# Gated delta rule inverse: levels 1 to 4 on 32 by 32 blocks in four places of the array, level 5 between blocks only

## Chip, cores, metric

One core of one Trainium2 chip runs the whole kernel in one launch. The metric is the device time in microseconds (us), of which the profile's span (first to last instruction) is nearly all.

## The reference, cut to what matters

The kernel computes six layers on 256 tokens of width 1024: a chain of four mixers (gated deltanet, HGRN2, GLA, gated deltanet), each followed by a SwiGLU block, and then two layers of another block. The change touches only the two gated deltanet ("gdn") layers, and in them only the inverse of a unit lower triangular matrix:

```
L = jnp.where(strict, jnp.einsum('bhncd,bhnsd->bhncs', kb, k) * decay, 0.0)
rhs = jnp.concatenate([v * beta[..., None], kb * jnp.exp(G)[..., None]], axis=-1)
sol = lax.linalg.triangular_solve(L + jnp.eye(CHUNK, dtype=F32), rhs, left_side=True, lower=True)
```

The kernel takes chunks of 128 tokens where the reference takes 64. So a gdn layer has 16 such matrices of 128 by 128: 8 heads times 2 chunks, numbered j, in four groups g of four.

## The kernel before

The inverse X of I + L is built by doubling. When X holds the inverses of the diagonal blocks of size 2^lv, level lv adds what couples two neighbours, by X - X C X, where C is L masked to that coupling (`level64`). Level 0 is I - C without a product. Levels 1 to 5 work on the two diagonal 64 by 64 blocks of each matrix. The two blocks lie on partitions 0 to 63 and 64 to 127 (`blocks`, line 336), so each product is issued twice, once for each block. Level 6 couples the two 64 blocks.

A level of one group g passes through the engines so:

- PE, line 894: C X, "cx", 4 matrices x 2 blocks = 8 matmuls into one PSUM bank.
- ACT, line 1427: copies the bank to `cx` (in `yb`).
- PE, `gdn_correct`, line 968: both X (CX) and its transpose, "z", 4 matrices x 2 forms x 2 blocks = 16 matmuls into one bank. X and its transpose XT are kept side by side in `inv` (`xx`).
- DVE, line 1903: subtracts the bank from X and XT, 128x512 at once. At level 5 it is three operations, and XT lands in the full-size matrices `inv[:, 16 + j, :]`, whose rest POOL has cleared (line 1415).
- POOL, line 1420: masks L for the next level into `lb_masked`, 4 matrices at a time, once cx of that group is done.

PE issues cx of group g and then z of group g - 1, so that ACT and DVE work on one group while PE works on another. At a level's start it issues cx of groups 0 and 1 and then waits for ACT's copy of group 0. Ahead of level 1, ACT copies the diagonal blocks of L to `lb`, POOL masks them, DVE forms XT of level 0, PE transposes it (line 949) and ACT copies it to X. Level 6 (lines 897 and 963) multiplies 64 by 64 blocks; behind it stand lines 907, 914 and 922, which apply the inverse to the values, on full 128 by 128 matrices.

A matmul in f32 is done in two passes; the trace has one record for the weight load and one for the product of each pass, so that x4 in a timeline row is two matmuls. Order is fixed by the program on each engine, and by semaphores between them. The function `stay_awake` issues products that nothing reads; there are none between levels 1 and 6.

Of the kernel before, what the change touches and what calls it, by code (L numbers as in the profile page):

```python
# [26 lines left out]
ALU = mybir.AluOpType  # L27
# [17 lines left out]
HALF2 = HALF // 2  # L45
TRI = 3 * HALF
# [166 lines left out]
def build(nc, A, out, book, layers=len(CHAIN)):  # L213

    book.restart()
    with ExitStack() as ctx:
# [47 lines left out]
        level64 = sb("level64", [P, 6, HALF2])  # L264
        ident64 = sb("ident64", [P, HALF2])

# [67 lines left out]

        cx = flat(yb)[:, 0:16 * HALF2].rearrange("p (j n) -> p j n", j=16)
        blocks = (slice(0, HALF2), slice(HALF2, HALF))
        xx = flat(inv[:, 0:16, :]).rearrange("p (g two j n) -> p g two j n", g=4, two=2, j=4)
        lb_masked, lb = (flat(ct)[:, 16 * HALF2 * n:16 * HALF2 * (n + 1)].rearrange("p (j n) -> p j n", j=16) for n in range(2))

        def inverse(j):  # L340


            return xx[:, j // 4, 0, j % 4, :]
# [151 lines left out]
        def _(pe):  # L495
# [353 lines left out]
            def gdn(layer):  # L849
# [34 lines left out]
                for lv in range(1, 7):  # L884
                    for g in range(4):
                        b = psum.claim(pe, "cx", layer, lv, g)
                        if lv < 6:
                            pe.wait_ge(*pool_gdn.at("masked", layer, lv, g))
                        pe.wait_ge(*(act_gdn.at("X", layer, g) if lv == 1 else dve_gdn.at("X", layer, lv - 1, g)))
                        for j in range(4 * g, 4 * g + 4):  # L890
                            cols_of = slice((j % 4) * HALF2, (j % 4 + 1) * HALF2)
                            if lv < 6:
                                for r in blocks:
                                    m = nc.tensor.matmul(b[r, cols_of], lb_masked[r, j, :], inverse(j)[r, :], start=True, stop=True)  # L894
                            else:
                                t0 = (j // 8) * T
                                m = nc.tensor.matmul(b[HALF2:HALF, cols_of], lt[0:HALF2, j % 8, t0 + HALF2:t0 + HALF], inverse(j)[0:HALF2, :],
                                                     start=True, stop=True)
# [44 lines left out]
            def gdn_transpose(layer, g):  # L943
# [3 lines left out]
                for j in range(4 * g, 4 * g + 4):  # L947
                    for r in blocks:
                        m = nc.tensor.matmul(b[r, (j % 4) * HALF2:(j % 4 + 1) * HALF2], transposed(j)[r, :], ident[r, r],
                                             start=True, stop=True)  # L950
                m.then_inc(*pe_gdn.tick("transposed", layer, g))

            def gdn_correct(layer, lv, g):
# [4 lines left out]
                if lv == 6:  # L958
                    pe.wait_ge(*dve_gdn.at("XT", layer, 5, g))
                for j in range(4 * g, 4 * g + 4):  # L960
                    c = (j % 4) * HALF2
                    if lv == 6:
                        m = nc.tensor.matmul(b[0:HALF2, c:c + HALF2], cx[HALF2:HALF, j, :], inv[HALF2:HALF, 16 + j, HALF2:HALF],
                                             start=True, stop=True)
                        continue
                    for left, right, c in ((transposed(j), cx[:, j, :], c), (cx[:, j, :], transposed(j), c + T)):
                        for r in blocks:
                            m = nc.tensor.matmul(b[r, c:c + HALF2], left[r, :], right[r, :], start=True, stop=True)  # L968
# [354 lines left out]
        def _(pool):  # L1323
# [83 lines left out]
            for layer, (kind, _) in enumerate(CHAIN[:layers]):  # L1407
# [7 lines left out]
                g.memset(inv[:, 16:32, 0:HALF2], 0.0).then_inc(*pool_gdn.tick("cleared", layer))  # L1415
                for lv in range(6):
                    for q in (0, 2, 1, 3) if lv == 0 else range(4):
# [3 lines left out]
                                        level64[:, lv:lv + 1, :].to_broadcast([P, 4, HALF2]), ALU.mult)\  # L1421
                            .then_inc(*pool_gdn.tick("masked", layer, lv, q))

        @block.scalar
        def _(act):
# [277 lines left out]
            def gdn(layer, l):  # L1703
# [16 lines left out]
                for g in (0, 2, 1, 3):  # L1720
                    act.wait_ge(*pe_gdn.at("transposed", layer, g))
                    run(s, group(g, 0), psum.bank("transposed", layer, g)[:, 0:T], ACT.Copy, "X", layer, g)
                    psum.release(s, "transposed", layer, g)
                for lv in range(1, 7):
                    for g in range(4):
                        act.wait_ge(*pe_gdn.at("cx", layer, lv, g))
                        rows_of = slice(0 if lv < 6 else HALF2, HALF)
# [886 lines left out]
```

## Time and profile before

| | us |
|---|---|
| median of 3 runs | 2289.57 |
| lowest and highest | 2284.36, 2289.63 |
| the profiled execution: its time | 2284.88 |
| its span | 2282.9 |
| mean granted TensorE clock over the span | 0.976 |

PE is matmuls, PEld weight loads, DVE the vector engine, ACT the scalar engine, POOL GpSimd. A stretch of the span is given as from:to in us from its start. The first gdn layer's inverse lies at 150 to 189, the second's at 1242 to 1281. "x" behind a busy time counts records.

### The profile page before, as it was taken

To read this page: it belongs to the slowest core of one execution; us is meant where nothing else is said; L and a number is where in the kernel's file an instruction comes from. 1 tells how busy PE (TensorE), PEld (TensorE's weight loads), DVE (VectorE), ACT (ScalarE), POOL (GpSimd) and SP (SyncE) were. 2 spreads that over 40 slices of the span, in tenths; PEclk is the share of its full clock that TensorE was granted. 3 is DMA by queue.
4 is the path that set the end of the run, shared out by engine and by line. 5 is a ranking of instruction groups with operands and counts; after the bars stand their busy time and mean duration, and the time that the engine had idled before them with its cause. 6 is when DMAs were issued, how large, how long until landed. Compare 5 with 4: busy or idle time off the path is not lost.

```text
span 2282.9 us, 35627 instructions
## 1 busy us (share of the span) xinstructions
PE 2172.9 (95%) x14401; PEld 1878.3 (82%) x14401; DVE 1497.0 (66%) x1925; ACT 883.7 (39%) x1153; POOL 210.2 (9%) x176
## 2 busy tenths in 40 slices
PE   7999999999999999999899999989789998979999
PEld 7988788898788788888798878869379997748998
DVE  6857654778744748554785664454677886367887
ACT  2243444232344322444314344444553334554332
POOL 5720000000000000000272100000210000030000
PEclk9999999999999999999999999999889999979999
DMA  7511655551555543665451165536025554403552
GB/s 213 182 41 57 203 185 186 175 184 46 201 185 185 167 155 99 198 193 168 148 185 57 39 209 186 184 117 196 1 84 180 190 174 138 137 10 129 185 184 93
DMA packets 265605, 333.81 MB, mean 146 GB/s; under 512 B 16492, under 2 KB 228593, under 8 KB 265473
## 3 DMA queue, kind: packets, MB, share of 16 engines
q1 hardware_dynamic: 265473, 331.93, 45.1%
q8 instruction: 98, 1.61, 0.3%
q14 instruction: 34, 0.28, 0.1%
HBM read 330.84 MB, written 1.05 MB: 145 GB/s over the span
## 4 chain that ended last, share of the span: by engine, by line
PE 86%; DVE 6%; ACT 4%; issue 2%; POOL 1%; SPq 0%; DMA 0%; POOLq 0%; DVEq 0%; ACTq 0%
PE bank L550 44%; PE bank L522 28%; PE bank L968 2%; PE bank L594 2%; PE bank L1023 1%; PE bank L584 1%; PE bank L741 1%; PE bank L894 1%; ACT w_hi L1473 1%; ACT stat L1427 1%; ACT mats L1427 1%; ACT xh L1427 1%; PE bank L847 1%; PE bank L833 1%; DVE xt L1913 1%
## 5 line engine op out<-in xcount | busy, mean ns | idle before, releaser
L1949 DVE TENSOR_TENSOR w_lo<-ring,w_hi 128x2048 fp32r<-128x2048 f32 (+2 forms) x297 | 627.6, 2115 | 356.9 <-ACT w_hi L1473 354.3
L1473 ACT ACTIVATE w_hi<-ring 128x2048 fp32r<-128x2048 f32 (+1 forms) x222 | 417.8, 1882 | 485.4 <-PE bank L550 302.2
L550 PE MATMUL bank<-w_lo,xh 128*128 128x512 f32 x992 | 268.7, 393 | 0.0
L550 PE MATMUL bank<-w_hi,xh 128*128 128x512 f32 x928 | 251.1, 392 | 10.6 <-ACT xh L1427 6.8
L550 PE MATMUL bank<-w_hi,xl 128*128 128x512 f32 x928 | 249.0, 390 | 0.0
L522 PE MATMUL bank<-xh,w_hi 128*128 128x256 f32 (+1 forms) x1816 | 243.6, 288 | 4.7 <-DVE w_hi L1947 4.7
L522 PE MATMUL bank<-xh,w_lo 128*128 128x256 f32 (+2 forms) x1880 | 245.3, 283 | 0.0
L522 PEld LDWEIGHTS bank<-xh,w_hi 128*128 128x128 f32 (+1 forms) x1816 | 230.7, 193 | 11.7 <-issue 4.5
L522 PE MATMUL bank<-xl,w_hi 128*128 128x256 f32 (+1 forms) x1816 | 237.2, 283 | 0.0
L522 PEld LDWEIGHTS bank<-xh,w_lo 128*128 128x128 f32 (+2 forms) x1880 | 232.1, 188 | 2.2 <-issue 0.2
L522 PEld LDWEIGHTS bank<-xl,w_hi 128*128 128x128 f32 (+1 forms) x1816 | 225.7, 190 | 0.7
L550 PEld LDWEIGHTS bank<-w_lo,xh 128*128 128x128 f32 x992 | 186.1, 189 | 38.1
L550 PEld LDWEIGHTS bank<-w_hi,xh 128*128 128x128 f32 x928 | 173.4, 189 | 49.9 <-issue 11.6
L550 PEld LDWEIGHTS bank<-w_hi,xl 128*128 128x128 f32 x928 | 174.7, 188 | 36.7
L1386 POOL TENSOR_TENSOR w_lo<-ring,w_hi 128x1536 fp32r<-128x1536 f32 x28 | 112.5, 4017 | 998.6 <-DVE w_hi L1947 998.6
L550 PE MATMUL bank<-w_hi,hid_hi 128*128 128x512 f32 x528 | 169.2, 402 | 8.1 <-DVE hid_lo L1903 8.1
L550 PE MATMUL bank<-w_hi,hid_lo 128*128 128x512 f32 x528 | 164.9, 394 | 0.0
L550 PE MATMUL bank<-w_lo,hid_hi 128*128 128x512 f32 x528 | 164.3, 393 | 0.0
L1427 ACT ACTIVATE yb<-bank 128x256 f32<-128x256 f32 (+4 forms) x146 | 59.0, 404 | 180.2 <-PE bank L550 125.0
L550 PEld LDWEIGHTS bank<-w_hi,hid_lo 128*128 128x128 f32 x528 | 100.2, 190 | 21.9
L550 PEld LDWEIGHTS bank<-w_lo,hid_hi 128*128 128x128 f32 x528 | 100.0, 189 | 21.9
L550 PEld LDWEIGHTS bank<-w_hi,hid_hi 128*128 128x128 f32 x528 | 95.5, 191 | 26.7 <-DVE hid_lo L1903 10.7
(314 smaller groups left out, 2504.4 us busy)
## 6 DMA issues: line engine op xcount, KB each, us to landing
ring<-in_ffn_w_in_dram SPq DMA_DIRECT2D x264, 512.0 KB, 4.4
ring<-in_ffn_w_down_dram SPq DMA_DIRECT2D x88, 512.0 KB, 4.2
ring<-in_gdn_w_in_dram SPq DMA_DIRECT2D x64, 512.0 KB, 5.0
ring<-in_ffn_w_out_dram SPq DMA_DIRECT2D x44, 512.0 KB, 3.9
ring<-in_w_in_dram SPq DMA_DIRECT2D x36, 512.0 KB, 4.7
ring<-in_hgrn_w_in_dram SPq DMA_DIRECT2D x32, 512.0 KB, 4.6
ring<-in_gla_w_in_dram SPq DMA_DIRECT2D x24, 512.0 KB, 4.7
ring<-in_gdn_w_out_dram SPq DMA_DIRECT2D x16, 512.0 KB, 4.1
```

The source lines that it names most:

```text
L522: m = nc.tensor.matmul(cols, *((wk, xk) if tokens == ALL else (xk, wk)), start=(first and step == 0 and k == 0 and (j % 2 == 0)), stop=(la ...
L550: m = nc.tensor.matmul(bank[:, 0:width], xin[:, k0 + k, rows_of], w[:, k, c * width:(c + 1) * width], start=(first and step == 0 and k == ...
L584: m = nc.tensor.transpose(b[:, j * P:(j + 1) * P], src[:, t, c * CHUNK + j * P:c * CHUNK + (j + 1) * P], ident[:, :])
L594: m = nc.tensor.matmul(b[:, 0:T], ones[:, :], strict[:, 0:T], start=True, stop=True)
L741: m = nc.tensor.transpose(banks[6][:, j * T + t * HALF:j * T + (t + 1) * HALF], hidt[:, t, j * P:(j + 1) * P], ident[:, :])
L833: nc.tensor.matmul(b[:, 0:T], k[:, 0:HALF], q[:, :], start=True, stop=True)
L847: nc.tensor.matmul(b[:, :], ones[:, :], gsq(g), start=True, stop=True).then_inc(*pe_gdn.tick("qk2", layer, g))
L968: m = nc.tensor.matmul(b[r, c:c + HALF2], left[r, :], right[r, :], start=True, stop=True)
L1386: g.tensor_tensor(w_lo[:, unit % RING, part], ring[:, unit % RING, part], high_part(unit)[:, part], ALU.subtract).then_inc(*pool_lo.tick())
L1427: nc.scalar.activation(out_, in_, func, **kw).then_inc(*sig.tick(*key))
L1473: nc.scalar.activation(high_part(u)[:, 0:n], ring[:, u % RING, 0:n], ACT.Copy).then_inc(*act_hi.tick())
L1949: v.tensor_tensor(w_lo[:, u % RING, 0:share], w[:, 0:share], high[:, 0:share], ALU.subtract).then_inc(*dve_lo.tick())
```

## The change

Levels 1 to 4 now work on the four diagonal 32 by 32 blocks of a matrix (`blocks` has four entries, and `level32`, `ident32` and `lb` are half as wide). Each product is issued four times, at rows and columns 0, 32, 64 and 96 of the array. The banks, copies, masks and subtractions of these levels cover half as many columns.

Level 5 computes only what lies between two 32 blocks of a 64 block. cx: 8 matmuls of 32 by 32 for a group, straight from `lt`, without a mask. z: 12 matmuls, three for each matrix. ACT copies two 32x128 pieces of a group, DVE writes three pieces of 32x128, one of them into a new full 64 by 64 place for X, `x64`, and two into the full-size XT.

The diagonal 32 blocks are brought to those places by POOL: six copies behind level 4, on which cx of level 6 waits ("assembled"). POOL no longer masks for level 5, and clears 128x2048 and 32x16x32 values where it cleared 128x1024.

On PE, in level 1, group 0's z before:

```order
113 L968 MATMUL bank<-yb,inv 64x64 x2
114 L968 MATMUL bank<-inv,yb 64x64 x2
115 L968 MATMUL bank<-yb,inv 64x64 x2
116 L968 MATMUL bank<-inv,yb 64x64 x2
117 L968 MATMUL bank<-yb,inv 64x64 x2
```

and now, at the same place:

```order
112 L900 MATMUL bank<-inv,ct 32x32 x32
113 L980 MATMUL bank<-yb,inv 32x32 x4
114 L980 MATMUL bank<-inv,yb 32x32 x4
115 L980 MATMUL bank<-yb,inv 32x32 x4
116 L980 MATMUL bank<-inv,yb 32x32 x4
```

Nothing changed places; there are twice as many matmuls, each of a quarter of the elements. On PE at level 5 and the start of level 6, now (L903 is cx, L974 and L976 are z, L906 is cx of level 6):

```order
261 L903 MATMUL bank<-inv,mats 32x32 x8
262 L974 MATMUL bank<-yb,inv 32x32
263 L976 MATMUL bank<-inv,yb 32x32 x2
...
285 L974 MATMUL bank<-yb,inv 32x32
286 L976 MATMUL bank<-inv,yb 32x32 x2
287 L906 MATMUL bank<-inv,mats 64x64 x8
```

The last of level 5 is followed at once by cx of level 6, as before. On POOL, the first layer's inverse before:

```order
44 L1415 MEMSET inv 128x16x64
45 L1420 TENSOR_TENSOR ct<-ct,level 128x256 x24
```

and now:

```order
44 L1427 MEMSET inv 128x2048
45 L1428 MEMSET inv 32x16x32
46 L1433 TENSOR_TENSOR ct<-ct,level 128x128 x20
47 L1439 COPY inv<-inv 32x16x32 x2
48 L1441 COPY inv<-inv 32x16x32 x4
```

Four masks are gone, and six copies stand behind the rest. The diff, cut to its core:

```diff
-        level64 = sb("level64", [P, 6, HALF2])
+        level32 = sb("level32", [P, 5, BLOCK])
...
-        blocks = (slice(0, HALF2), slice(HALF2, HALF))
+        cx64 = flat(yb)[:, 8 * HALF:8 * HALF + 16 * HALF2].rearrange("p (j n) -> p j n", j=16)
+        blocks = [slice(BLOCK * n, BLOCK * (n + 1)) for n in range(4)]
+        pairs = (blocks[0], blocks[1]), (blocks[2], blocks[3])
+        xx = flat(inv[:, 0:8, :]).rearrange("p (g two j n) -> p g two j n", g=4, two=2, j=4)
+        x64 = flat(inv[:, 8:16, :]).rearrange("p (j n) -> p j n", j=16)
...
-                        if lv < 6:
+                        if lv < 5:
                             pe.wait_ge(*pool_gdn.at("masked", layer, lv, g))
+                        if lv == 6:
+                            pe.wait_ge(*pool_gdn.at("assembled", layer))
...
+                            elif lv == 5:
+                                for of, to in pairs:
+                                    m = nc.tensor.matmul(b[to, n * BLOCK:(n + 1) * BLOCK], lt[of, j % 8, t0 + to.start:t0 + to.stop],
+                                                         inverse(j)[of, :], start=True, stop=True)
...
-                if lv == 6:
-                    pe.wait_ge(*dve_gdn.at("XT", layer, 5, g))
...
+                    elif lv == 5:
+                        r = blocks[1]
+                        m = nc.tensor.matmul(b[r, c:c + BLOCK], transposed(j)[r, :], cx[r, j, :], start=True, stop=True)
+                        for to, r in pairs:
+                            m = nc.tensor.matmul(b[to, c + HALF:c + HALF + BLOCK], cx[r, j, :], transposed(j)[r, :], start=True, stop=True)
...
-                g.memset(inv[:, 16:32, 0:HALF2], 0.0).then_inc(*pool_gdn.tick("cleared", layer))
-                for lv in range(6):
+                g.memset(inv[:, 16:32, :], 0.0).then_inc(*pool_gdn.tick())
+                g.memset(x64[blocks[0], :, BLOCK:HALF2], 0.0).then_inc(*pool_gdn.tick("cleared", layer))
+                for lv in range(5):
...
+                pool.wait_ge(*dve_gdn.at("X", layer, 4, 3))
+                for r in blocks[:2]:
+                    g.tensor_copy(x64[r, :, r].rearrange("p (g j) n -> p g j n", g=4), xx[r, :, 0, :, :]).then_inc(*pool_gdn.tick())
+                for r in blocks:
+                    g.tensor_copy(inv[r, 16:32, r].rearrange("p (g j) n -> p g j n", g=4), xx[r, :, 1, :, :])\
+                        .then_inc(*pool_gdn.tick("assembled", layer))
...
+                            for r in (slice(0, HALF),) if lv < 5 else (pairs[0][1], pairs[1][1]):
+                                run(s, flat(cx[r, 4 * g:4 * g + 4, :]), b[r, 0:HALF], ACT.Copy, "cx", layer, lv, g)
...
-                            tt(s, group(g, 0), group(g, 0), b[:, 0:T], ALU.subtract, "X", layer, lv, g)
-                            for r in blocks:
-                                tt(s, inv[r, 16 + 4 * g:16 + 4 * g + 4, r], xx[r, g, 1, :, :],
-                                   b[r, T:2 * T].rearrange("p (h n) -> p h n", h=4), ALU.subtract, "XT", layer, lv, g)
+                            dve.wait_ge(*pool_gdn.at("cleared", layer))
+                            r = blocks[1]
+                            ts(s, x64[r, 4 * g:4 * g + 4, blocks[0]], b[r, 0:HALF].rearrange("p (h n) -> p h n", h=4), -1.0, ALU.mult)
+                            for to, r in pairs:
+                                ts(s, inv[to, 16 + 4 * g:16 + 4 * g + 4, r], b[to, HALF:T].rearrange("p (h n) -> p h n", h=4),
+                                   -1.0, ALU.mult, None, None, "X", layer, lv, g)
```

## Rows read from the trace of the kernel before

**Rows 1.** The page: busy us (share) xinstructions; the chain that ended last.
```profile
PE 2172.9 (95%) x14401; PEld 1878.3 (82%) x14401; DVE 1497.0 (66%) x1925; ACT 883.7 (39%) x1153; POOL 210.2 (9%) x176
...
PE 86%; DVE 6%; ACT 4%; issue 2%; POOL 1%; SPq 0%; DMA 0%; POOLq 0%; DVEq 0%; ACTq 0%
```

**Rows 2.** Stretches: length, busy PE, PEld, DVE, ACT, POOL, clock, DMA, GB/s.
```profile
150.00:154.64 4.64, 4.03 (x74) 3.36 (x74) 2.21 (x4) 2.81 (x7) 3.17 (x5) 1.00 0.00 0
154.64:178.88 24.24, 23.71 (x776) 23.09 (x772) 10.28 (x15) 6.54 (x17) 12.79 (x19) 1.00 0.02 4
178.88:185.31 6.43, 5.91 (x196) 5.66 (x193) 3.58 (x10) 1.54 (x4) 0.00 (x0) 1.00 0.01 3
185.31:189.10 3.79, 3.74 (x77) 3.48 (x74) 3.08 (x8) 1.52 (x4) 0.00 (x0) 1.00 0.02 4
1246.40:1271.24 24.84, 24.04 (x775) 23.29 (x772) 10.33 (x15) 6.53 (x17) 12.76 (x18) 1.00 0.02 4
1271.24:1276.96 5.72, 5.62 (x193) 5.51 (x190) 3.50 (x9) 1.54 (x4) 0.00 (x0) 1.00 0.02 6
1276.96:1280.80 3.84, 3.79 (x80) 3.53 (x75) 3.11 (x8) 1.52 (x4) 0.00 (x0) 1.00 0.00 0
```

**Rows 3.** Timeline of PE in level 2 (start, length, x passes).
```profile
162.28 0.33 PE L968 MATMUL bank<-yb,inv 64*64 64x64 f32 x4
...
163.23 0.66 PE L894 MATMUL bank<-inv,ct 64*64 64x64 f32 x16
```

**Rows 4.** Timeline of PE where level 5 meets level 6.
```profile
185.36 0.22 PE L968 MATMUL bank<-yb,inv 64*64 64x64 f32 x1
185.42 0.22 PE L897 MATMUL bank<-inv,mats 64*64 64x64 f32 x1
185.42 0.22 PE L968 MATMUL bank<-inv,yb 64*64 64x64 f32 x2
185.48 0.22 PE L897 MATMUL bank<-inv,mats 64*64 64x64 f32 x1
185.48 0.22 PE L968 MATMUL bank<-inv,yb 64*64 64x64 f32 x1
185.53 0.92 PE L897 MATMUL bank<-inv,mats 64*64 64x64 f32 x13
```

**Rows 5.** Timeline at the start of level 2, PE and ACT.
```profile
161.05 1.13 PE L894 MATMUL bank<-inv,ct 64*64 64x64 f32 x32
...
161.75 0.85 ACT L1427 ACTIVATE yb<-bank 128x256 f32<-128x256 f32 x2 [2.39 <-PE bank L894]
```

**Rows 6.** Groups by shape, ACT and DVE (xcount | busy us, mean ns | idle).
```profile
L1427 ACT ACTIVATE yb<-bank 128x256 f32<-128x256 f32 x128 | 49.2, 384 | 166.8 <-PE bank L550 125.0 <-PE bank L894 40.8
L1427 ACT ACTIVATE ct<-bank 128x512 f32<-128x512 f32 x8 | 4.8, 598 | 9.7 <-PE bank L922 5.3 <-PE bank L907 4.3
L1903 DVE TENSOR_TENSOR inv<-inv,bank 128x512 f32<-128x512 f32 x32 | 22.0, 688 | 30.2 <-PE bank L968 30.2
L1907 DVE TENSOR_SCALAR inv<-bank 64x256 f32<-64x256 f32 x8 | 3.3, 417 | 1.5 <-PE bank L963 1.2
```

**Rows 7.** Groups by shape: POOL.
```profile
L1420 POOL TENSOR_TENSOR ct<-ct,level 128x256 f32<-128x256 f32 x48 | 34.8, 740 | 52.7 <-ACT ct L1427 31.2 <-PE bank L894 21.2
L1396 POOL TENSOR_TENSOR sq<-sq,trig 128x512 f32<-128x512 f32 x4 | 5.6, 1395 | 686.5 <-PE bank L1104 686.5
L1415 POOL MEMSET inv<- 128x1024 f32 x2 | 1.9, 951 | 48.7 <-ACT dec L1427 48.7
```

**Rows 8.** Stretches with PE nearly idle, and what followed.
```profile
1104.60:1107.49 2.89, 0.00 (x0) 0.00 (x0) 2.85 (x5) 2.40 (x2) 0.00 (x0) 1.00 0.73 238
1107.49:1114.32 6.83, 4.34 (x19) 2.88 (x20) 5.48 (x9) 1.69 (x4) 0.00 (x0) 0.50 0.00 0
2046.40:2048.20 1.80, 0.16 (x4) 0.11 (x4) 1.76 (x4) 0.19 (x1) 1.57 (x1) 1.00 0.00 0
```

**Rows 9.** DMA queues, 154.6 to 185.3: packets, MB, share of 16 engines.
```profile
q8 instruction: 7, 0.11, 1.8%
```

More of the change, by code:

```diff
@@ L45 @@
 HALF2 = HALF // 2
+BLOCK = HALF2 // 2
 TRI = 3 * HALF
@@ L333, in u @@
             return ct[:, 8 * t + h, :]
-        cx = flat(yb)[:, 0:16 * HALF2].rearrange("p (j n) -> p j n", j=16)
-        blocks = (slice(0, HALF2), slice(HALF2, HALF))
-        xx = flat(inv[:, 0:16, :]).rearrange("p (g two j n) -> p g two j n", g=4, two=2, j=4)
-        lb_masked, lb = (flat(ct)[:, 16 * HALF2 * n:16 * HALF2 * (n + 1)].rearrange("p (j n) -> p j n", j=16) for n in range(2))
+        cx = flat(yb)[:, 0:16 * BLOCK].rearrange("p (j n) -> p j n", j=16)
+        cx64 = flat(yb)[:, 8 * HALF:8 * HALF + 16 * HALF2].rearrange("p (j n) -> p j n", j=16)
[3 more added lines that the diff above has]
+        x64 = flat(inv[:, 8:16, :]).rearrange("p (j n) -> p j n", j=16)
+        lb_masked, lb = (flat(ct)[:, 16 * BLOCK * n:16 * BLOCK * (n + 1)].rearrange("p (j n) -> p j n", j=16) for n in range(2))
         def inverse(j):
@@ L1721, in gdn @@
                     act.wait_ge(*pe_gdn.at("transposed", layer, g))
-                    run(s, group(g, 0), psum.bank("transposed", layer, g)[:, 0:T], ACT.Copy, "X", layer, g)
+                    run(s, group(g, 0), psum.bank("transposed", layer, g)[:, 0:HALF], ACT.Copy, "X", layer, g)
                     psum.release(s, "transposed", layer, g)
@@ L1726, in gdn @@
                         act.wait_ge(*pe_gdn.at("cx", layer, lv, g))
-                        rows_of = slice(0 if lv < 6 else HALF2, HALF)
-                        run(s, flat(cx[rows_of, 4 * g:4 * g + 4, :]), psum.bank("cx", layer, lv, g)[rows_of, 0:T], ACT.Copy,
-                            "cx", layer, lv, g)
+                        b = psum.bank("cx", layer, lv, g)
+                        if lv == 6:
+                            run(s, flat(cx64[HALF2:HALF, 4 * g:4 * g + 4, :]), b[HALF2:HALF, 0:T], ACT.Copy, "cx", layer, lv, g)
+                        else:
+                            for r in (slice(0, HALF),) if lv < 5 else (pairs[0][1], pairs[1][1]):
+                                run(s, flat(cx[r, 4 * g:4 * g + 4, :]), b[r, 0:HALF], ACT.Copy, "cx", layer, lv, g)
                         psum.release(s, "cx", layer, lv, g)
@@ L2276, in gdn @@
                             X = xx[:, g, :, :, :].rearrange("p two j n -> p (two j n)")
[L2277 removed]
+                            tt(s, X, X, b[:, 0:T], ALU.subtract, "X", layer, lv, g)
                         elif lv == 5:
[L2279 to L2282 removed]
+                            dve.wait_ge(*pool_gdn.at("cleared", layer))
[4 more added lines that the diff above has]
+                                   -1.0, ALU.mult, None, None, "X", layer, lv, g)
                         else:
```

37 lines of the change are left out of this document (18 added, 19 removed).

## The prediction, made before the changed kernel ran

> **What bounds the kernel now.** I read the page's busy times and its chain first, then the busy time of each engine by stretch, then the timeline inside one level. PE is busy for 95% of the span and makes up 86% of the chain that ended last [rows 1], so a change on PE counts where it stands. In levels 1 to 4 PE is busy 23.71 of 24.24 us in the first layer and 24.04 of 24.84 in the second, at the full clock, with DVE under half and POOL at about half [rows 2]. A level takes 24.54 / 4 = 6.1 us on average of both layers. Level 5 takes 6.43 and 5.72 us, level 6 3.79 and 3.84 [rows 2]. The stage is bound by the pace of PE's passes, and all that it saves should reach the end, since PE is the bound behind it too.
>
> The pace: 32 passes of z start from 162.28 to 163.23, 0.0297 us each, 0.059 us for a matmul of two passes [rows 3]. A level has 96 matmuls: 5.7 us, and 0.4 is left for the wait at its start. Where only one place of the array is in use, 13 passes of level 6 take 0.92 us, the last of them 0.22 us long: (0.92 - 0.22) / 12 = 0.058 us a pass [rows 4]. So two places at once halve the time of a pass: a place is busy 0.058 us with 64 columns, and two places don't disturb each other.
>
> **Levels 1 to 4.** They have twice the matmuls, 192 a level, each 32 columns wide in one of four places. How long such a pass holds its place isn't in the trace. If it goes with the columns, it is 0.029 us; four places at once then give 0.0073 us a pass and 0.015 us a matmul. That is the lower end. The upper end within this mechanism is the shortest mean distance at which passes are seen to start: where three places are in use, three start within 0.06 us (at 185.42 twice in L968 and once in L897, then again at 185.48) [rows 4], so 0.0195 us a pass and 0.039 us a matmul. But those three stand within 0.01 us of each other and the rest is the place being busy, so issue isn't what spaced them. I take 0.020 us a matmul, nearer the lower end for that reason: 192 x 0.020 = 3.84 us.
>
> To this comes the wait at a level's start. Before, cx of groups 0 and 1 is issued from 161.05, so group 0's last pass starts at about 161.5; ACT starts its copy at 161.75, two copies take 0.85 us [rows 5], and z starts at 162.28 [rows 3], 0.8 us after group 0's last pass and 0.3 us after group 1's. Now ACT copies 128 columns: from 384 ns at 256 columns and 598 at 512 [rows 6] I work out 0.28 us, so z can start 0.68 us after group 0's last pass, of which group 1's cx covers 16 x 0.020 = 0.32. The wait is 0.36 us. All other waits are covered: DVE's subtraction of 256 columns takes 0.42 us (417 ns for 256, 688 for 512 [rows 6]), and between a z and the cx that needs it PE has at least 2 us of other groups; POOL's mask of 128 columns takes at most the 0.74 us of 256 [rows 7], 3.0 us for four against 4.2. A level is then 3.84 + 0.36 = 4.2 us, four are 16.8, against 24.54: 7.7 us less for a layer.
>
> PE's code has to be fetched too. From 154.6 to 185.3 there are 7 instruction packets in 1.8% of 16 engines' 30.7 us [rows 9], 1.26 us each, for some 450 matmuls, so 64 to a packet. 768 matmuls need 12 packets, 15.1 us: under 16.8, if they follow each other directly. The Trainium skill says how large they are ("Runtime: NRT & Kernel Launch", section Instruction fetch mechanics): blocks of 256 instructions, fetched while the others run, hidden by an issue floor of about 20 cycles an instruction. By that floor four instructions for a matmul would take longer than the 0.059 us that the trace shows now, so the trace doesn't agree with the floor, and the cover that the page speaks of may go.
>
> **Ahead of level 1.** ACT's copies of the last diagonal blocks double in number at 0.28 instead of about 0.4 us each: 1.1 instead of 0.8 us for a group, so 0.7 later over the last two. Against it stand POOL's shorter masks (two, up to 0.25 each), DVE's subtraction (0.14 less), and 64 transposes at 0.020 instead of 32 at 0.059: 0.6 less. I take 0.3 us less; bounds 0.6 less and 0.7 more. The longer clearing costs nothing: POOL idles 48.7 us ahead of the two it has now, and they take 0.95 us each [rows 7].
>
> **Levels 5 and 6.** PE's part shrinks from 96 to 80 matmuls, in two places or one: a z group of 12 holds its busiest place for 4 x 2 x 0.029 = 0.23 us, as long as cx. All together PE has 1.9 us, with waits for ACT's eight copies (2.2 us) 3.3 us. DVE's twelve pieces at 0.28 us are 3.4 us and end 5 us after level 5 began, though only the last group's are needed late. But now level 6 waits for POOL. X of level 4's last group is ready 0.7 us after cx of level 5 starts (z ends, 0.25 to DVE, 0.42 for it), and then come six copies of 512 values in each of 32 partitions. The trace has no POOL copy. Its bounds are half of clearing 1024 values, 0.48 us, and the product of two inputs of 512 values, 1.40 us [rows 7]. I take 0.85, between them, since a copy reads one input where the product reads two. So level 6 starts at 0.75 + 6 x 0.85 = 5.85 us, rounded up to 6.0 for the waits on both sides; bounds 5.0, where DVE is last, and 9.2. Level 6 itself stays at 3.8 us: 9.8 against 10.22 and 9.56 before, mean 9.9. So what level 5 saves on PE turns into a wait for POOL: 0.1 less.
>
> **The clock.** PE has nothing to do from 3.3 to 6.0 us, 2.7 us. In the trace a granted clock of 1.00 fell to 0.50 behind 2.89 us without a pass, for 6.83 us, and stayed at 1.00 behind 1.80 us in which PE was busy 0.16 [rows 8]. 2.7 us with a thin stretch ahead lies nearer the first, so I take the fall to half, the level at 1.2 GHz. Up to 3.4 of the 6.83 us are lost then; level 6 and what follows are bound by PE for some 0.7 of the time, so 2.4 us more for a layer (bounds 0 and 3.4).
>
> **The sum.** A layer: -7.7 - 0.3 - 0.1 + 2.4 = -5.7 us; both -11.4. The profiled execution of 2284.9 us would be 2273.5, its span 2271.5. That execution lies 4.7 us under the median of 2289.57, so beside the median the forecast is 2278.2 us, 0.5% less.
>
> **Rivals.** The first: the clock doesn't fall. Then it is -8.1 a layer, 2273.4 us. For it: the gap is somewhat shorter than the 2.89 us.
>
> The second: POOL eats the gain. With 1.40 us a copy level 6 starts 3.2 us later in each layer, and the clock falls for certain with up to 1.0 us more: -11.4 + 8.4 gives 2286.6 us, no change that can be told. For it: nothing in the trace shows a strided copy of 32-wide pieces. Against it: the 1.40 us belong to two inputs. The same time results if a matmul costs 0.030 us in the levels (0.010 x 192 x 4 = 7.7 us a layer, less the shorter wait).
>
> The third ends slower: the starts of passes have a spacing of their own on PE, however many places are free. It decides from the point where four levels lose the 5.7 us: (22.5 / 4 - 0.36) / 192 = 0.0274 us a matmul, 0.0137 a pass. The trace shows no mean under 0.0195 [rows 4]. With that as the spacing, a level is 192 x 0.039 + 0.3 = 7.8 us, four are 31.2, 6.7 more than before; with +2 for the rest of the layer it is about 2307 us. The same mechanism at its worst is that the four places don't work at once at all, so that the change doesn't do what its words say: 4 x 0.0073 = 0.029 us a pass, as now with two, 0.058 a matmul, 11.5 us a level, 2289.6 + 2 x (21.5 + 2) = 2337 us. Against it speaks that passes for different places start within 0.01 us of each other [rows 4].
>
> The Trainium skill has such a rule ("TensorE: Matmul & The Clock Gate", section Wait — 56ns, not 53.3ns?): start to start never drops under about 25 ns, however narrow the product. The starts that lie closer in the rows speak against it holding between places. By that figure, as an estimate, a level would take some 10 us and the kernel about 2325 us. Its section on packing small matmuls says the opposite, a start each 4 ns between places.
>
> **How the numbers follow.** The forecast's mechanism, with the clock falling in at least one of the layers, has 0.42; the clock staying up, 0.18; POOL or the pace eating the gain, 0.20; the third rival 0.20. The measurement of this kernel tells 0.3% from no change, so faster is under 2282.7 us and slower over 2296.4. Faster has the first two, 0.60, same 0.21, slower 0.19. The range leaves out most of the third rival and reaches from 2264 (0.015 us a matmul, 13.2 us for four levels, though fetching holds it at 15.1; POOL at its lower bound; no fall of the clock: -1.7 beyond -8.1 for the pace and -1.0 for POOL in each layer, and some margin) to 2294 (POOL's upper bound and a pace of 0.025 together).
>
> **What would show it.** In the changed profile: four levels in 16.8 us and z passes for four places starting within 0.04 us; ACT's copies of 128 columns at 0.28 us; six POOL copies of 0.85 us behind level 4 with cx of level 6 right behind the last; DVE done before it; the granted clock at 0.5 in about 187 to 194. The prediction is wrong if levels take over 22 us, if a POOL copy takes over 1.2 us, or if level 6 waits for another engine.

## The result, and the profile after

The changed kernel takes 2335.2 us (median of 4 runs, 2332.5 to 2337.0) beside 2288.9 us for the kernel before in the same comparison: a ratio of 1.0206, with a 95% interval of 1.0188 to 1.0223. It is slower by 2.1%, far outside the spread of either kernel. The forecast was 2278.2 us with a range of 2264 to 2294, so the sign is wrong and the time lies outside the range.

The page after shows the busy time and share of each engine, the queue of instruction packets, and the chain that ended last. Its first and last line answer to [rows 1]; the packets' line of the page before stands below.

```profile
PE 2177.7 (93%) x16001; PEld 1877.8 (81%) x16001; DVE 1484.8 (64%) x1929; ACT 883.5 (38%) x1177; POOL 200.3 (9%) x182
...
q8 instruction: 111, 1.82, 0.3%
...
PE 84%; DVE 7%; ACT 4%; issue 4%; POOL 1%; SPq 0%; DMA 0%; DVEq 0%; POOLq 0%; ACTq 0%
```

```profile
q8 instruction: 98, 1.61, 0.3%
```

PE is busy hardly longer than before (2177.7 us against 2172.9), although the run is 46 us longer. What grew in the chain is "issue", time in which PE waited for nothing that the profile shows: from 2% to 4%. Instruction packets went from 98 to 111 for 800 more matmuls (half of the 1600 more records), which fits 64 matmuls a packet. The loss is small on the page because the page averages over the whole span. Stretch by stretch it can't be missed. These rows answer to [rows 2], with the same columns: ahead of level 1, levels 1 to 4 in two pieces, level 5, level 6, what follows, and then levels 1 to 4, 5 and 6 of the second layer.

```profile
150.00:154.30 4.30, 3.18 (x138) 2.54 (x139) 1.52 (x4) 3.07 (x11) 1.87 (x5) 1.00 0.00 0
154.30:165.00 10.70, 5.10 (x374) 4.67 (x362) 1.26 (x3) 1.39 (x5) 2.46 (x6) 0.63 0.02 5
165.00:200.84 35.84, 18.74 (x1181) 17.21 (x1184) 5.05 (x12) 3.32 (x12) 3.57 (x8) 0.50 0.02 4
200.84:206.26 5.42, 3.68 (x181) 3.27 (x172) 2.69 (x9) 2.15 (x8) 3.63 (x6) 0.50 0.03 6
206.26:212.05 5.79, 5.79 (x70) 5.62 (x65) 2.39 (x7) 1.51 (x4) 0.00 (x0) 0.50 0.00 0
212.05:220.00 7.95, 7.95 (x54) 7.80 (x54) 3.57 (x5) 2.33 (x4) 0.00 (x0) 0.81 0.01 2
1268.90:1315.70 46.80, 24.73 (x1566) 22.50 (x1551) 6.31 (x15) 4.71 (x17) 6.13 (x14) 0.51 0.02 4
1315.70:1321.20 5.50, 3.86 (x162) 3.46 (x161) 2.41 (x8) 2.15 (x8) 3.63 (x6) 0.50 0.01 3
1321.20:1327.00 5.80, 5.80 (x69) 5.62 (x65) 2.67 (x8) 1.51 (x4) 0.00 (x0) 0.50 0.01 3
```

Levels 1 to 4 take 46.5 us (the second and third row) where they took 24.24, and 46.8 where they took 24.84. PE is busy for only 23.8 of the 46.5 us, and no other engine is busy for more than a seventh of it. So PE waits half the time, and not for ACT, DVE or POOL. Level 5 is shorter (5.4 and 5.5 us against 6.43 and 5.72). Level 6 is longer (5.8 against 3.8), with PE busy all of it at a granted clock of 0.50. From the start of level 1 to the end of level 6 the layers take 23.3 and 23.7 us more than before. That is 47 of the 49.4 us by which the span grew from 2282.9 to 2332.3. The rest lies mostly just behind level 6, while the clock is still down: the matmuls behind the inverse (L550 before, L554 now) start 24.3 us later in the first layer (232.64 against 208.36), 1.3 more than the offset at the end of level 6.

Next, who had PE waiting. The first fence has groups of PE over levels 1 to 4 of the first layer (count | busy us, mean ns | idle us before them and what ended it), the second single rows of the timeline in that stretch.

```profile
L980 PE MATMUL bank<-inv,yb 32*32 32x32 f32 x506 | 17.4, 235 | 10.6 <-issue 10.6
L980 PE MATMUL bank<-yb,inv 32*32 32x32 f32 x511 | 17.0, 235 | 10.2 <-issue 9.9 <-ACT yb L1447 0.2
L900 PE MATMUL bank<-inv,ct 32*32 32x32 f32 x512 | 9.5, 231 | 1.9 <-issue 1.9
```

```profile
154.32 0.77 PE L900 MATMUL bank<-inv,ct 32*32 32x32 f32 x63
...
157.90 0.27 PE L980 MATMUL bank<-yb,inv 32*32 32x32 f32 x4 [2.17 <-issue]
...
188.66 0.21 PE L980 MATMUL bank<-yb,inv 32*32 32x32 f32 x1 [2.18 <-issue]
...
189.22 1.09 PE L900 MATMUL bank<-inv,ct 32*32 32x32 f32 x64
...
192.78 0.26 PE L980 MATMUL bank<-yb,inv 32*32 32x32 f32 x2 [1.90 <-issue]
...
196.49 0.26 PE L980 MATMUL bank<-yb,inv 32*32 32x32 f32 x2 [1.79 <-issue]
...
200.29 0.27 PE L980 MATMUL bank<-yb,inv 32*32 32x32 f32 x3 [1.86 <-issue]
```

22.4 of the 22.7 us of idle time end with "issue". They come as twelve gaps of 1.5 to 2.2 us, one every 3.6 to 4.1 us, in the middle of a group of matmuls where no wait is written. Between the gaps the passes are fast: 63 of them start within 0.77 - 0.19 = 0.58 us at full clock (9 ns each), and 64 within 1.09 - 0.24 = 0.85 us at half clock (13.5 ns each). So the four places do work at once. The queue of instruction packets over the same stretch, as [rows 9]:

```profile
q8 instruction: 12, 0.20, 1.8%
```

Twelve packets in 46.2 us are one every 3.85 us, for 64 matmuls each, and the gaps have the same period. The share gives 0.018 x 16 x 46.2 / 12 = 1.1 us a packet, but that is time added up over the DMA engines that work on it together. Two packets in slices of 0.1 us (the last two columns are the share of the 16 DMA engines and GB/s), and the gaps that follow them in the chain (start, length):

```profile
163.40:163.50 0.10, 0.10 (x17) 0.10 (x10) 0.10 (x1) 0.00 (x0) 0.00 (x0) 0.50 0.60 164
166.90:167.00 0.10, 0.10 (x25) 0.10 (x13) 0.00 (x0) 0.10 (x1) 0.10 (x1) 0.50 0.65 164
```

```profile
163.65 2.03 issue
...
167.89 1.46 issue
```

A packet's 16 KB all move within 0.1 us (164 GB/s), and in the slices of 0.1 us beside these nothing moves. Over the twelve gaps, the bytes of a packet move 1.0 to 1.8 us after PE came out of the gap before, and PE comes out of the next one 2.2 to 2.8 us after them (165.68 for the first packet shown, 169.35 for the second). So the 3.85 us are not time in which data moves. What else they are spent on, the trace doesn't show.

### The profile page after: what moved, and what is told of

It reads as the page before. It is cut to its first block, busy times and chain, and to the rows that moved or that the text cites. A ratio compares the mean times of both kernels' runs of the same rounds, so it can differ in the third digit from the quotient of the medians.

```text
span 2332.3 us, 38871 instructions
## 1 busy us (share of the span) xinstructions
PE 2177.7 (93%) x16001; PEld 1877.8 (81%) x16001; DVE 1484.8 (64%) x1929; ACT 883.5 (38%) x1177; POOL 200.3 (9%) x182
## 4 chain that ended last, share of the span: by engine, by line
PE 84%; DVE 7%; ACT 4%; issue 4%; POOL 1%; SPq 0%; DMA 0%; DVEq 0%; POOLq 0%; ACTq 0%
PE bank L554 43%; PE bank L526 27%; PE bank L980 1%; PE bank L598 1%; PE bank L1035 1%; PE bank L588 1%; ACT stat L1447 1%; PE bank L745 1%; ACT xh L1447 1%; PE bank L900 1%; ACT w_hi L1493 1%; ACT mats L1447 1%; PE bank L851 1%; DVE w_lo L1972 1%; DVE xt L1936 1%
## 5 line engine op out<-in xcount | busy, mean ns | idle before, releaser
L554 PE MATMUL bank<-w_lo,xh 128*128 128x512 f32 x992 | 267.4, 391 | 0.0
L554 PE MATMUL bank<-w_hi,xh 128*128 128x512 f32 x928 | 250.7, 392 | 11.1 <-ACT xh L1447 7.4
L554 PE MATMUL bank<-w_hi,xl 128*128 128x512 f32 x928 | 249.0, 390 | 0.0
L554 PEld LDWEIGHTS bank<-w_lo,xh 128*128 128x128 f32 x992 | 185.6, 188 | 37.8
L554 PEld LDWEIGHTS bank<-w_hi,xh 128*128 128x128 f32 x928 | 173.0, 188 | 50.2 <-issue 11.6
L554 PEld LDWEIGHTS bank<-w_hi,xl 128*128 128x128 f32 x928 | 174.8, 188 | 36.7
L554 PE MATMUL bank<-w_hi,hid_hi 128*128 128x512 f32 x528 | 169.0, 401 | 8.1 <-DVE hid_lo L1926 8.1
L554 PE MATMUL bank<-w_hi,hid_lo 128*128 128x512 f32 x528 | 165.0, 394 | 0.0
L554 PE MATMUL bank<-w_lo,hid_hi 128*128 128x512 f32 x528 | 164.4, 393 | 0.0
L1447 ACT ACTIVATE yb<-bank 128x256 f32<-128x256 f32 (+6 forms) x154 | 56.8, 369 | 228.6 <-PE bank L554 124.9
L1970 DVE CAST w_hi<-ring 128x2048 fp32r<-128x2048 f32 x75 | 93.3, 1244 | 38.7 <-ACT pj L1447 17.8
L554 PEld LDWEIGHTS bank<-w_lo,hid_hi 128*128 128x128 f32 x528 | 100.3, 190 | 21.9
L554 PEld LDWEIGHTS bank<-w_hi,hid_lo 128*128 128x128 f32 x528 | 100.0, 189 | 21.9
```

Source lines behind the costliest of these rows:

```text
L554: m = nc.tensor.matmul(bank[:, 0:width], xin[:, k0 + k, rows_of], w[:, k, c * width:(c + 1) * width], start=(first and step == 0 and k == ...
L1447: nc.scalar.activation(out_, in_, func, **kw).then_inc(*sig.tick(*key))
L1970: v.tensor_copy(high[:, 0:n], w[:, 0:n]).then_inc(*dve_hi.tick())
```

## The experiments

**Theory A**: the fetch of PE's instructions sets the pace of levels 1 to 4, one packet of 64 f32 matmuls every 3.85 us. **Theory B**: the clock, at half from 157.1 us on, makes the levels long. **Theory C**: the four places of the array hinder each other, or small tiles do.

**A loop in place of straight code, on 32 by 32 blocks.** TensorE's code for one level is written once and run three times; the waits are the same but for one that was over long before, and their values rise with the turn. ScalarE's, VectorE's and GpSimd's code is as it was.

```diff
+                level(1)
+                with pe.Fori(0, 12, 4) as turn:
+                    level(2, turn)
...
-                pe.wait_ge(*act_gdn.at("cx", layer, lv, g))
+                wait_all(waits, turn)
```

> The changed kernel with TensorE's code for level 2 in a hardware loop of three turns, which runs levels 2, 3 and 4; the same 576 matmuls are run on the same tiles and the waits are the same, but the code of two of three of these levels is not fetched again. Theory A (the fetch of TensorE's instructions sets the pace of levels 1 to 4: one packet of 16 KB, 64 f32 matmuls, every 3.86 us, 0.060 us a matmul): level 1 and the loop's first turn keep 11.6 us each, the second and third turn take 3 to 5.1 us (192 matmuls are 384 passes, at 7.5 ns with the clock full and 13.4 ns with the clock at half), so levels 1 to 4 take 29 to 33.5 us in place of 46.5, and the run 2301 to 2310 us. Theory B (the clock at half is what makes the levels long): each turn stays at 11.6 us, the run at 2335. Theory C (the four places of the array hinder each other): as B.

Measured: 2311.8 us, ratio 1.0105 (1.0083 to 1.0127), 23.4 us less than the changed kernel, and 1.8 more than theory A's upper figure. Stretches, from ACT's first copy of a level to its first copy of the next, for levels 1, 2, 3 and 4:

```profile
155.23:166.32 11.09, 5.83 (x399) 5.40 (x388) 1.69 (x4) 1.11 (x4) 1.91 (x5) 0.61 0.02 4
166.32:178.63 12.31, 6.87 (x405) 6.14 (x400) 1.68 (x4) 1.11 (x5) 1.81 (x4) 0.50 0.02 5
178.63:184.19 5.56, 5.06 (x391) 4.74 (x383) 1.68 (x4) 1.11 (x5) 1.80 (x4) 0.73 0.00 0
184.19:188.83 4.64, 4.36 (x383) 4.04 (x383) 1.68 (x4) 1.11 (x5) 0.00 (x0) 1.00 0.00 0
```

The same instructions on the same tiles take 12.31 us in the loop's first turn and 5.56 in its second. The last columns show why: in the first two rows code is fetched, in the last two nothing moves. Theory C falls, since nothing about tiles or places differs between the turns. Also the clock is back at 1.00 in the third turn, once PE hardly waits. The four levels add up to 33.6 us, at the upper end of the 29 to 33.5 expected.

**The same loop on the kernel before.**

> The kernel before with TensorE's code for level 2 in a hardware loop of four turns, which runs levels 2 to 5. Theory A: there the 64 matmuls of a packet take 3.74 us by themselves and the packet 3.86, so the fetch was just not the limit or just the limit: the levels stay at 24.2 us or lose at most 0.12 us for each of the packets no longer fetched (about 5 in a layer), together 2287 to 2289 us, same as before. If the levels get shorter by more than 1 us a layer, the passes at 64 by 64 were not the limit of the kernel before either.

Measured: 2289.0 us beside 2286.6, ratio 1.0008 (0.9994 to 1.0022). Levels 1 to 4:

```profile
154.88:179.12 24.24, 23.79 (x776) 23.15 (x773) 10.94 (x16) 6.15 (x17) 12.08 (x17) 1.00 0.01 2
```

24.24 us in both: on 64 by 64 blocks the passes set the pace, not the fetch. The two were close, though: the passes of 64 matmuls take 128 x 0.0297 = 3.8 us [rows 3], 4.0 with the waits (24.24 / 6), and the changed kernel got a packet every 3.85. The kernel before sat right at a limit that it didn't show.

**Twice the instructions on 64 by 64 blocks.** Each matmul of levels 1 to 5 becomes two of 32 columns.

```diff
-  m = nc.tensor.matmul(b[r, c:c + HALF2], left[r, :], right[r, :], ...)
+  for c1 in (0, HALF2 // 2):
+      m = nc.tensor.matmul(b[r, c + c1:c + c1 + HALF2 // 2], left[r, :], right[r, c1:c1 + HALF2 // 2], ...)
```

> The kernel before with each matmul of levels 1 to 5 on 64 by 64 blocks written as two of 32 columns: the same columns pass on the same two places, the instructions are twice as many. Theory A: 768 matmuls at 0.060 us are 46.1 us for levels 1 to 4 in place of 24.2, and level 5 takes 11.5 in place of 6.4: 27 us more a layer, the run at about 2343 us (2335 to 2350). Theory C, or any in which small blocks or four places of the array are at fault: the levels stay near 24 us, the run at 2289 to 2295.

Measured: 2341.8 us, ratio 1.0242 (1.0223 to 1.0261), inside theory A's figures. But the number is right and the reason isn't:

```profile
155.08:200.88 45.80, 45.49 (x1545) 45.17 (x1541) 10.98 (x16) 6.14 (x17) 11.74 (x17) 1.00 0.02 4
```

PE is busy for 45.49 of 45.80 us at full clock. It never waits for code. 1545 passes in 45.80 us are 0.0296 us each, just what a pass of 64 columns took [rows 3]. So a pass on a 64 by 64 place holds it for 0.059 us with 32 columns too, and 64 matmuls then take 3.8 us by themselves, by chance the period of the fetch. The run says nothing for or against theory A. It does show that the time between passes doesn't go with their columns here; whether the product or the weight load (PEld, busy for 45.17 us too) sets it, the run doesn't separate.

**Fillers in the levels.** One matmul of 128 by 128 by 256, whose result nobody reads, behind each group.

> The changed kernel with one filler matmul of 128 by 128 by 256 behind each group of levels 1 to 4: 16 more matmuls in a layer (1 us by 0.060 us each), about 6 us more busy time, to hold the clock up. Theory A: levels 1 to 4 keep 46 to 49 us even if the clock stays at 1.00, and only level 6 and what is behind it come back to their full pace (3.8 in place of 5.8, 2.05 in place of 3.5 us): 2328 to 2340 us. Theory B: with the clock full the levels fall to 25 to 31 us, the run to about 2300.

Measured: 2336.6 us, ratio 1.0216 (1.0197 to 1.0235). Levels 1 to 4, then level 5:

```profile
157.06:204.27 47.21, 38.88 (x1562) 26.91 (x1564) 6.65 (x16) 4.45 (x16) 5.62 (x13) 0.68 0.02 5
204.27:209.67 5.40, 4.36 (x154) 3.99 (x150) 3.50 (x13) 2.15 (x8) 3.64 (x6) 0.50 0.01 3
```

PE is busy for 15 us more and the clock is higher (0.68 for 0.52), and the levels take the same time: 47.2 us, against 46.7 for the changed kernel between the same two copies. So the waits took in the fillers' work, and theory B falls. In the changed kernel the first gap opens before the clock falls, too: PE is idle for 2.17 us up to 157.90 (row above), and a mean clock of 0.63 over 10.7 us from 154.30 puts the fall at 157.1. One part of the expectation missed: the clock was down again in level 5, so nothing was won behind it (level 6 took 5.8 us).

**All four levels in the loop**, and the same with a filler behind each group of level 5.

> The changed kernel with TensorE's code for one level in a hardware loop of four turns, which runs levels 1 to 4. Theory A (fetch, 3.86 us for each 64 matmuls): only the first turn is fetched, 11.6 us; the others take 4.6 to 5.6 us as turns two and three did in e1_loop32. Levels 1 to 4 take 25.4 to 28 us, 6 to 7 us a layer less than there, the run 2298 to 2301 us: still above the kernel before, whose 24.2 us need no more than its passes. If something other than the fetch made level 1 long (the first use of small tiles, the clock), it stays: 2311 us.

> e5_loopall32 with one filler matmul of 128 by 128 by 256 behind each group of level 5. If the idle time of TensorE in level 5 is what lets the clock fall there, level 6 comes back from 5.8 to 3.8 us and u0 from 3.5 to 2.05, less up to 1.6 us for the fillers: 2 to 4 us a layer less than e5_loopall32, 2291 to 2297. If the clock falls for the thin work and not for the idle time, the run is 0 to 3 us longer than e5_loopall32.

Measured: 2299.0 us, ratio 1.0059 (1.0038 to 1.0080), and 2295.5 us, ratio 1.0046 (1.0024 to 1.0068). Levels 1 to 6 of the first:

```profile
157.44:168.56 11.12, 6.53 (x397) 5.76 (x401) 1.69 (x4) 1.11 (x5) 1.81 (x4) 0.56 0.02 4
168.56:174.38 5.82, 5.34 (x389) 5.05 (x386) 1.68 (x4) 1.11 (x5) 1.81 (x4) 0.66 0.00 0
174.38:179.43 5.05, 4.45 (x392) 4.04 (x396) 1.69 (x4) 1.11 (x5) 1.82 (x4) 1.00 0.00 0
179.43:184.07 4.64, 4.37 (x383) 4.04 (x383) 1.69 (x4) 1.10 (x5) 0.00 (x0) 1.00 0.00 0
184.07:189.26 5.19, 3.80 (x152) 3.47 (x147) 3.40 (x12) 2.15 (x8) 3.63 (x6) 0.70 0.01 3
189.26:195.00 5.74, 5.74 (x61) 5.57 (x60) 1.67 (x4) 1.51 (x4) 0.00 (x0) 0.50 0.01 3
```

and levels 5 and 6 of the second:

```profile
184.69:190.37 5.68, 5.45 (x164) 3.67 (x165) 3.11 (x11) 2.15 (x8) 3.63 (x6) 1.00 0.01 3
190.37:194.30 3.93, 3.84 (x62) 3.53 (x60) 1.96 (x6) 1.51 (x4) 0.00 (x0) 1.00 0.00 0
```

Only the first turn costs 11 us; levels 1 to 4 are 26.6 us, 20 less than in the changed kernel and still 2.4 more than before. Fillers in level 5 cost 0.5 us there and give back 1.8 in level 6: the clock falls for PE's idle time in level 5, as the forecast said, and was held here by work nobody needs. In the first run the wait for POOL that the forecast names is seen too, but short: PE idles 0.74 us and starts cx of level 6 at 188.14, 0.10 us behind POOL's last copy.

**Level 5 alone.** The kernel before with the second part of the change only, and the same with the fillers.

```diff
+                    if lv == 5:
+                        c = (j % 4) * BLOCK
+                        r = quarters[1]
+                        m = nc.tensor.matmul(b[r, c:c + BLOCK], transposed(j)[r, BLOCK:HALF2], cx32[r, j, :], ...)
+                        for to, r in pairs:
+                            m = nc.tensor.matmul(b[to, c + HALF:c + HALF + BLOCK], cx32[r, j, :], transposed(j)[r, BLOCK:HALF2], ...)
```

> The kernel before with only the second part of the change: levels 1 to 4 on 64 by 64 blocks as before, level 5 computes what lies between the 32 by 32 blocks (80 matmuls of 32 columns in place of 96 of 64), GpSimd makes no mask for level 5 and copies the blocks on the diagonal in 4 copies. Theory A (this part is harmless and small): level 5 takes 4.8 to 5.4 us in place of 6.4, GpSimd's copies (4 of 0.65 us) end before level 6 begins, the run is 2 to 3 us shorter than before: 2283.5 to 2285. Rival: TensorE idles more in level 5, the clock falls to half behind it, and level 6 and the first matmuls behind it take 3.5 us more a layer: 2290 to 2292.

> e6_level5 with one filler matmul of 128 by 128 by 256 behind each group of level 5. In e6_level5 the clock was at half for 13.7 us from level 5 on and level 6 took 5.7 us. If TensorE's idle time in level 5 lets it fall, the fillers hold it at full, level 6 is back at 3.8 us, and the run is 3 to 6 us shorter than e6_level5: 2287 to 2291. If the fillers only cost, it is 2296 to 2298.

Measured: 2294.9 us, ratio 1.0041 (1.0025 to 1.0056), and with fillers 2285.2 us, ratio 0.9999 (0.9987 to 1.0010). Levels 5 and 6 without and with fillers:

```profile
178.86:184.83 5.97, 3.94 (x153) 3.46 (x147) 3.72 (x13) 2.15 (x9) 2.44 (x4) 0.69 0.01 3
184.83:190.50 5.67, 5.67 (x61) 5.50 (x60) 1.67 (x4) 1.51 (x4) 0.00 (x0) 0.50 0.01 3
```

```profile
179.21:184.86 5.65, 5.42 (x164) 3.65 (x165) 3.41 (x12) 2.15 (x8) 2.42 (x4) 1.00 0.02 6
184.86:188.80 3.94, 3.85 (x62) 3.54 (x60) 1.97 (x6) 1.51 (x4) 0.00 (x0) 1.00 0.00 0
```

The rival had the right mechanism: with work left out of level 5, PE idles for 2 of 6 us, the clock falls, and level 6 takes 1.7 us longer than with fillers. The run is 3 us above the rival's figures all the same, and with fillers it falls by 9.7 us, more than the 3 to 6 expected. PE's longest idle stretch in this level 5 is again one that no engine ends:

```profile
183.21 0.21 PE L978 MATMUL bank<-yb,inv 32*32 32x32 f32 x1 [1.34 <-issue]
```

It lies in the middle of a group, and the packet before it moved at 180.7, 2.5 us before its end, as in the levels above. So it looks like the fetch too: the 80 narrow matmuls use up their code faster than it comes. No run tests that.

What the edit costs is read where the matmuls behind the inverse start. In the profiled executions that is 2.8 us later than in the kernel before in the first layer (211.13 against 208.36), and 4.8 us later in the second (1304.81 against 1300.05). With fillers it is 207.44 and 1296.94, 7.9 us earlier than without in the second. So about 5 of the 9.9 us over the kernel before, and 7.9 of the fillers' gain, lie in the two inverses and just behind them. In the profiled executions another 7.5 us lie in a stage that the edit doesn't touch. It is the same work of 158 passes, first in the kernel before, then in this one:

```profile
1600.00:1661.00 61.00, 45.21 (x158) 25.96 (x159) 33.97 (x76) 36.03 (x93) 16.20 (x14) 0.78 0.00 1
```

```profile
1605.00:1673.50 68.50, 55.70 (x158) 29.47 (x159) 32.99 (x76) 36.31 (x93) 15.58 (x14) 0.63 0.00 0
```

The clock is lower there, and executions of the kernel before alone range from 2279.7 to 2293.0 us. Between the same two matmuls around that stage the profiles differ without regard to level 5: 71.0 us in the kernel before, 76.7 in its loop (which leaves level 5's matmuls as they are), 80.3 here, but 73.6 in the changed kernel, which has the same level 5. So that share is not shown to come from the edit.

**A third fewer instructions.** If each matmul costs 0.060 us whatever it does, work that moves off TensorE pays even if another engine is slower at it. Here VectorE makes the transposed inverse by its transpose of 32 by 32 blocks: 128 matmuls a level in place of 192, and none of the 64 ahead of level 1.

```diff
-                            X = xx[:, g, :, :, :].rearrange("p two j n -> p (two j n)")
-                            tt(s, X, X, b[:, 0:T], ALU.subtract, "X", layer, lv, g)
+                            tt(s, group(g, 0), group(g, 0), b[:, 0:HALF], ALU.subtract, "X", layer, lv, g)
...
+                            dve.wait_ge(*s.now())
+                            v.transpose(group(g, 1), group(g, 0)).then_inc(*s.tick("XT", layer, lv, g))
```

> The changed kernel with the transposed inverse made by VectorE's transpose of 32 by 32 blocks (four of 128 by 128 in a level and four ahead of level 1) and not by TensorE: levels 1 to 4 hold 512 matmuls in place of 768, the 64 that transposed ahead of level 1 are gone, all of it straight code. Theory A (0.060 us for each matmul, whatever it does): levels 1 to 4 take 31 us in place of 46.5 and up to 3.8 us more are saved ahead of them, 15.5 to 19 us a layer, the run at 2297 to 2304 us. If the passes, the clock or the small tiles set the pace, VectorE's added step keeps the levels near 46 us, 2335.

> As e10_dve_straight, with TensorE's code for a level in a loop of four turns (as e5_loopall32), 128 matmuls a turn, two packets. Theory A: the first turn is fetched in 7.5 to 7.8 us, the others take 2.3 to 3.5 us (256 passes at 7.5 ns are 1.9 us; the chain through ScalarE and twice VectorE is about 2.3), levels 1 to 4 15 to 18 us in place of 25.4 to 27 in e5_loopall32 and of 24.2 before: 8 to 11 us a layer less than e5_loopall32, the run at 2276 to 2284 us, below the kernel before. Rival: VectorE's added step sets the pace of a turn at 4.6 us or more, the run at 2288 to 2292.

> e8_dve_transpose with one filler matmul of 128 by 128 by 256 behind each group of level 5, as e7_loopall_awake. There the fillers kept the clock full behind level 5 and the run was 3 us shorter. The same here: 2273 to 2281 us; if the clock is half already when level 5 begins, no gain: as e8_dve_transpose.

Measured: straight code 2302.4 us, ratio 1.0076 (1.0050 to 1.0101). In the loop 2280.5 us, ratio 0.9979 (0.9967 to 0.9991). In the loop with fillers in level 5 2276.7 us, ratio 0.9960 (0.9947 to 0.9974), beside 2285.8 for the kernel before. Levels 1 to 4 of the straight code:

```profile
155.87:184.68 28.81, 15.83 (x1018) 14.75 (x1019) 8.93 (x31) 4.44 (x16) 5.95 (x14) 0.56 0.02 5
```

and the four turns of the loop without fillers:

```profile
156.88:162.47 5.59, 4.54 (x274) 4.14 (x267) 2.31 (x8) 1.11 (x5) 1.82 (x4) 0.50 0.01 3
162.47:166.81 4.34, 3.93 (x260) 3.56 (x254) 2.28 (x8) 1.10 (x4) 1.81 (x4) 0.67 0.02 4
166.81:170.78 3.97, 3.38 (x263) 2.91 (x267) 2.32 (x8) 1.11 (x5) 1.81 (x4) 1.00 0.00 0
170.78:174.31 3.53, 3.34 (x255) 2.94 (x256) 2.12 (x8) 1.11 (x5) 0.00 (x0) 1.00 0.00 0
```

The straight code went from 46.7 us for 768 matmuls to 28.8 for 512: 0.061 and 0.056 us each, so the time follows the count of instructions, at a little less than the 31 us expected. The packets keep their period: 8 from 154 to 184.7, one every 3.84 us. PE is still idle for 13 of the 28.8 us. With the loop the four levels take 17.4 us against 24.25 before. With loop and fillers the kernel beats both others: it is 9.1 us below the one before, 0.4%, a small gain but clear of zero. VectorE's transposes take 0.31 us each, and PE idles for only 0.2 to 0.6 us in a turn behind the first, so waiting for them costs at most that. Still the turns missed the expected 2.3 to 3.5 us: 4.34, 3.97 and 3.53, the first of these with the clock partly down. The first turn took 5.59 us where 7.5 to 7.8 were expected: only one of its two packets came within it (at 158.2), and none from 150 on before that, so the code of the other was there already. It ran at half the clock, which had begun to fall ahead of it: with the 64 transposing matmuls gone, PE did nothing from 153 to 156.

## Why the prediction was wrong, point by point

**What bounds the kernel** was right for the kernel before: PE bounded the stage, and what happened to it there reached the end in full (47 of 49.4 us). In the changed kernel PE's code bounds the stage, and no longer its passes.

**Levels 1 to 4: the step that failed** is the one on PE's code, "12 packets, 15.1 us: under 16.8, if they follow each other directly". They don't. The 1.26 us come from a share of 16 DMA engines [rows 9]: they are the busy time of all engines on a packet, neither how long a packet is under way (its bytes move within 0.1 us) nor how often one can come, and I took them for the latter. The period is 3.85 us, so 12 packets need 46 us and not 15. The loop shows it in one kernel: 12.31 us with the fetch, 5.56 without. The Trainium skill ("Runtime: NRT & Kernel Launch", section Instruction fetch mechanics) says that the fetch hides behind the issue of instructions. Here it doesn't: PE is idle for 22.4 us with nothing else to wait for. The prediction noted that the trace doesn't agree with the floor which that needs, and said that the cover may go, but then priced the case where it goes with the 1.26 us alone. The row to look at was there: seven packets in 30.7 us, one every 4.4 us, in a stretch where 64 matmuls took 4.0 us. It doesn't tell how much faster packets could come, and so the price of twice as many was unknown, not 15.1 us: such a resource is one to test before doubling the demand. (The "some 450 matmuls" of that step are 486 by the records of [rows 2]; 64 to a packet was right all the same.)

**The pace of the passes** was right where code was at hand. I took 0.020 us a matmul. The bursts show 9 ns a pass, 0.018, and a level without fetching 4.64 us, where I had 4.2. The assumption under it, that a pass's time goes with its columns, was wrong and did no harm: the split matmuls took 0.059 us for 32 columns on 64 by 64, and with 32 columns on 32 by 32 a place gets a pass every 4 x 9 = 36 ns. The rule of the Trainium skill ("TensorE: Matmul & The Clock Gate", section Wait — 56ns, not 53.3ns?) that starts never lie closer than about 25 ns does not hold between places, where they lie 9 ns apart.

**The third rival** had the right size at its worst, 11.5 us a level and 2337 us, by the wrong mechanism: the places do work at once. A reader who sees 2335 would take it for confirmed. The gaps of 2 us between fast bursts, and nothing even about the starts, are what tells the two apart. Its 2307 and my 0.20 for the whole group had nothing of the fetch in them.

**ACT, DVE and POOL.** ACT's copy of 128 columns took 277 ns (0.28 forecast), DVE's 256 columns 421 ns (0.42), its pieces 284 ns (0.28). POOL's copies, the term with the widest bounds, were cheaper than I took them:

```profile
201.76 1.26 POOL L1439 COPY inv<-inv 32x512 f32<-32x512 f32 x2 [15.89 <-DVE inv L1926]
203.08 2.60 POOL L1441 COPY inv<-inv 32x512 f32<-32x512 f32 x4
```

They take 0.61 us each (607 and 602 ns in the groups), 0.65 from start to start, in place of 0.85. Level 6 starts 5.4 us after level 5 does, not 6.0, and the forecast's wait for POOL isn't what sets that in the changed kernel: POOL's last copy ends at 205.68, and cx of level 6 starts at 206.26, right behind z of level 5's last group. PE's longest idle stretch in level 5 is not 2.7 us for POOL but 0.94 us up to 204.13, with "issue" behind it. The term for levels 5 and 6 without the clock, -0.1 us, came out at -0.6 for level 5 on the mean of both layers.

**Ahead of level 1** the forecast had -0.3, and level 1 starts 0.3 us earlier in the first layer (154.30 against 154.64). That isn't shown to be the change: with level 5 alone changed, ACT's first copy of level 1 comes 0.4 us earlier as well (154.98 against 155.39).

**The clock** fell to 0.50, the level at 1.2 GHz, but in level 1 and not behind level 5: PE idled half of every 4 us there, and the fall came within the first gap. It stayed down to about 215 us, 58 us in all (0.81 over the 7.95 us from 212.05 on). It cost little inside the levels, where PE waited anyway, then 2.0 us in level 6 (5.8 against 3.8) and 1.3 more behind it in the first layer. I had +2.4 a layer, so the size was near, by luck in part: the fall came from the fetch in level 1 and not from the wait for POOL. The two runs with fillers in level 5 show that idle time in level 5 has the forecast's effect where the levels themselves keep PE busy.

## What to carry to other kernels

Count instructions as a resource of their own when a change trades large instructions for many small ones. Read how often code packets come, not how long one takes, and compare that period with the time that the instructions of one packet will need: in this kernel, below some 3.85 us for 64 f32 matmuls the fetch was the bound, however fast the array is. The share of a queue in the DMA engines' time says nothing about that period. Then a hardware loop over the repeated part, or moving a share of the instructions to another engine, is worth more than faster ones; both together, with fillers in level 5, turned a loss of 2.1% into a gain of 0.4%. And work left out on the engine that bounds a kernel is only saved if what is behind it is ready: otherwise the idle time may cost the clock.

## What the runs showed of the hardware that I had not expected

- TensorE's straight code comes in packets of 16 KB, 64 f32 matmuls, one every 3.85 us: 12 (0.20 MB) in the 46.2 us of the changed kernel's levels. The bytes of one move within 0.1 us, with 0.60 to 0.91 of the 16 DMA engines busy in that slice. PE goes on 2.2 to 2.8 us after them. With 15 us more of PE's work beside it the stretch was as long.
- A loop's code is not fetched again: 0.00 in the share of DMA in turns 2 to 4 on 32 by 32 blocks, with bodies of 192 matmuls. With a body of 128 one packet came in turn 2 (at 165.7) and none in turns 3 and 4; what it held isn't shown.
- A pass on a 64 by 64 place holds it for 0.059 us with 32 columns as with 64. On 32 by 32 places 64 passes start 9 ns apart at full clock and 13.5 at half.
- The granted clock was 0.52 over the changed kernel's four levels, where PE was busy for 24.0 of 46.7 us, and 0.69 over the new level 5 in the kernel before, busy for 3.94 of 5.97 us. In the loop over all four levels it was 1.00 in turns 3 and 4, busy for 4.45 of 5.05 and 4.37 of 4.64 us. So 32 by 32 work does not lower it by itself.
- VectorE's transpose of 128 by 128 values as 32 by 32 blocks takes 0.31 us. GpSimd's copy of 512 values in each of 32 partitions takes 0.61.
